# The first unit of an up projection by whole products instead of by seven half products, and other buffers for the first loads of the down projection

## The reference

```python
x = x + merged @ w_out                               # output projection
h = rms_norm(x, ffn_norm_g)
u, v = jnp.split(h @ w_up, 2, axis=-1)               # 2 x 5632 columns
u = causal_dwconv(u, conv_w, conv_b)                 # 3 taps over the tokens
x = x + (jax.nn.gelu(u) * v) @ w_down                # down projection
return rms_norm(x, final_norm_g)
```

## Time and profile before

| what | value |
|---|---|
| median of 3 runs | 2808.55 us (2808.36 to 2808.84) |
| the profiled execution, device time | 2806.89 us |
| its span in the trace | 2805.1 us |
| PE busy | 2751.3 us, 98% |
| DVE, ACT, POOL busy | 1509.0, 1008.1, 187.2 us |
| mean granted clock of TensorE | 0.992 |
| share of the chain of waits on PE | 93% |

### The profile page before, as it was taken

How to read it: one execution, slowest core, us unless ns; L and a number is a source line. 1 busy time by engine, 2 the same in 40 slices (tenths; PEclk the granted TensorE clock), 3 DMA queues, 4 the chain that set the end, 5 groups by cost and what they waited for, 6 DMA issues and landing times.

```text
span 2805.1 us, 40745 instructions
## 1 busy us (share of the span) xinstructions
PE 2751.3 (98%) x15945; PEld 2422.0 (86%) x15945; DVE 1509.0 (54%) x1831; ACT 1008.1 (36%) x1237; POOL 187.2 (7%) x156
## 2 busy tenths in 40 slices
PE   8999999999999999999989999999999998999998
PEld 6888888888888888888789999999999987888886
DVE  4445542233333433342487878787878864455454
ACT  4334432222232322132455444555554432122223
POOL 0003310000111000000000000000000000000002
PEclk9999999999999999999999999999999999999999
DMA  6532123334333233343434343535343434333332
GB/s 175 135 103 57 53 75 97 97 92 108 85 82 97 75 102 92 97 143 120 135 94 129 103 132 101 134 101 135 101 131 105 130 131 167 124 115 134 105 113 97
DMA packets 421668, 308.89 MB, mean 110 GB/s; under 512 B 6469, under 2 KB 367574, under 8 KB 420969
## 3 DMA queue, kind: packets, MB, share of 16 engines
q1 hardware_dynamic: 415351, 295.83, 36.7%
q10 hardware_dynamic: 5826, 10.76, 1.1%
q0 software_dynamic: 432, 1.50, 0.2%
HBM read 288.09 MB, written 22.06 MB: 111 GB/s over the span
## 4 chain that ended last, share of the span: by engine, by line
PE 93%; DVE 2%; issue 2%; ACT 1%; DMA 1%; SPq 0%; POOL 0%; ACTq 0%; DVEq 0%; POOLq 0%
PE bank L889 31%; PE bank L528 19%; PE bank L530 19%; PE bank L529 19%; PE bank L719 2%; PE bank L713 1%; DMA x_in<-in_x_dram 0%; DMA a_dram<-v_sb 0%; DVE ring_lo L1717 0%; ACT l_win L1081 0%; ACT l_slc L1081 0%; PE bank L769 0%; POOL l_slc L1952 0%; SPq L362 0%; PE bank L868 0%
## 5 line engine op out<-in xcount | busy, mean ns | idle before, releaser
L528 PE MATMUL bank<-h_hi,w_hi 128*128 128x512 f32 x1216 | 481.3, 396 | 2.8 <-DVE w_lo L1419 2.8
L530 PE MATMUL bank<-h_hi,w_lo 128*128 128x512 f32 x1216 | 474.6, 390 | 0.0
L529 PE MATMUL bank<-h_lo,w_hi 128*128 128x512 f32 x1216 | 474.3, 390 | 0.0
L889 PE MATMUL bank<-t_hi,ring_hi 128*128 128x256 f32 x1408 | 401.4, 285 | 18.6 <-DVE ring_lo L1717 18.6
L889 PE MATMUL bank<-t_hi,ring_lo 128*128 128x256 f32 x1408 | 400.5, 284 | 0.0
L1409 DVE TENSOR_TENSOR w_lo<-w_raw,w_hi 128x2048 fp32r<-128x2048 f32 x105 | 240.7, 2292 | 262.0 <-ACT w_hi L983 261.7
L983 ACT ACTIVATE w_hi<-w_raw 128x2048 fp32r<-128x2048 f32 x105 | 200.8, 1912 | 424.7 <-PE bank L530 420.6
L889 PE MATMUL bank<-m32r,ring_hi 128*128 128x256 f32 x1408 | 327.5, 284 | 0.0
L889 PEld LDWEIGHTS bank<-t_hi,ring_hi 128*128 128x128 f32 x1408 | 272.6, 194 | 19.6 <-issue 19.6
L528 PE MATMUL bank<-d_hi,a_hi 128*128 128x512 f32 x704 | 275.0, 391 | 7.9 <-DVE x L1889 7.9
L529 PE MATMUL bank<-d_lo,a_hi 128*128 128x512 f32 x704 | 274.7, 390 | 0.0
(11 more groups left out here) (283 smaller groups left out, 4883.1 us busy)
## 6 DMA issues: line engine op xcount, KB each, us to landing
w_raw<-in_w_in_dram SPq DMA_DIRECT2D x76, 1024.0 KB, 5.7
raw<-in_w_up_dram SPq DMA_DIRECT2D x44, 1024.0 KB, 6.9
raw<-in_w_up_dram SPq DMA_DIRECT2D x88, 512.0 KB, 6.2
d_raw<-in_w_down_dram SPq DMA_DIRECT2D x44, 1024.0 KB, 5.1
w_raw<-in_w_out_dram SPq DMA_DIRECT2D x16, 1024.0 KB, 5.1
a_dram<-v_sb SPq DMA_DIRECT2D x44, 256.0 KB, 2.0
a_in<-a_dram SPq DMA_DIRECT2D x11, 1024.0 KB, 7.4
w_raw<-in_w_branch_nsa_dram SPq DMA_DIRECT2D x8, 1024.0 KB, 5.7
```

What stands on the lines that cost most here:

```text
L528: mm(dst, l_hi, r_hi, start=first, stop=False)
L529: mm(dst, l_hi, r_lo, start=False, stop=False)
L530: return mm(dst, l_lo, r_hi, start=False, stop=final)
L889: last = mm(pb[bank][:, 0:TH], left[:, w], right[:, k, :], start=first and k == 0 and left is ring_hi[b] and right is y_hi, stop=k == KH - ...
```

## The change

- Unit 0 of the up projection becomes two whole slots, S_UP (the column of v) and S_UP + 1 (of u): 16 k-tiles by 3 matmuls of 512 columns each into banks 0 and 1. For it the whole m32 is split into h_hi and h_lo in quarters (h2_hi, h2_lo), three of them beside the last slots of the output projection. Products are now 7 x 43.
- y11, y21 and y22 are views of h_hi and h_lo. Only t1 to t4 are made by sums, and t3 and t4 lie in what is free by then. The first sum and t1's split stand beside the last output slot; the others stand in between on ScalarE and VectorE while TensorE runs unit 0 and the first products of unit 1.
- TensorE: eight k-tiles of v, the transposes of group 3, four of v, eight of u, the row scales, four of u, then the last four of each. SyncE: loads of unit 1, the two slots, then unit 2.
- The ring, the raw buffers, s_a, s_3, u_sb, v_sb, d_raw, d_hi, d_lo and the a buffers have other places. The first two quarters of x1 are loaded into buffers of their own (xs) before the last product ends.
- At the end of the up projection the piece for the last but one product comes ahead of the split of the first down slot on VectorE, and the split of the first a_in behind the last piece. The second a_in is loaded after the x1 quarters that have their own buffers.

The diff, cut to its core:

```diff
-S_DN = S_WO + 16
+S_UP = S_WO + 16
+S_DN = S_UP + 2
 UNITS = D_FF // P
-PRODUCTS = 7 * UNITS
+PRODUCTS = 7 * (UNITS - 1)
...
+    q, half = (0 if r <= 1 else 7 * r - 9), (r - 1) // 2
     if i is None:
-        return Unit(r, r, r // 2, 0 if r == 0 else 7 * r - 2)
-    return Unit(i * 4 + r, r, i * 2 + r // 2, i * 28 + (7 * r - 2))
+        return Unit(r, r, half, q)
+    return Unit(i * 4 + r, r, i * 2 + half, i * 28 + q)
...
-    h_hi = at("h_hi", 0, [P, KT, SEQ], F32R)
-    h_lo = at("h_lo", 32 * KB, [P, KT, SEQ], F32R)
+    hl = at("hl", 0, [P, 2, KT, SEQ], F32R)
+    h_hi, h_lo = hl[:, 0], hl[:, 1]
...
-    raw = [[at("raw00", A_, [P, 2, KH * P]), at("raw01", A_ + 8 * KB, [P, 2, KH * P])],
-           [at("raw10", 72 * KB, [P, 2, KH * P]), at("raw11", 88 * KB, [P, 2, KH * P])]]
-    ring_at = [A_ + 16 * KB, A_ + 24 * KB, 48 * KB, 56 * KB]
+    rs_rep2 = at("rs_rep2", A_ + 40 * KB, [P, TOK, P])
+    raw = [[at("raw00", 64 * KB, [P, 2, KH * P]), at("raw01", 72 * KB, [P, 2, KH * P])],
+           [at("raw10", A_ + 16 * KB, [P, 2, KH * P]), at("raw11", A_ + 24 * KB, [P, 2, KH * P])]]
+    ring_at = [A_ + 32 * KB, Y_, 80 * KB, 96 * KB]
     ring_hi = [at(f"ring_hi{b}", ring_at[b], [P, KH * P], F32R) for b in range(RING)]
     ring_lo = [at(f"ring_lo{b}", ring_at[b] + 4 * KB, [P, KH * P], F32R) for b in range(RING)]
-    s_a = [at(f"s_a{b}", A_ + 32 * KB + b * 4 * KB, [P, KH * P]) for b in range(2)]
-    s_3 = at("s_3", 64 * KB, [P, KH * P])
-    u_sb = at("u_sb", 68 * KB, [P, 2, SEQ])
-    v_sb = at("v_sb", 104 * KB, [P, 4, SEQ])
+    s_a = [at(f"s_a{b}", Y_ + 8 * KB + b * 4 * KB, [P, KH * P]) for b in range(2)]
+    v_sb = at("v_sb", 88 * KB, [P, 4, SEQ])
+    u_sb = at("u_sb", 104 * KB, [P, 2, SEQ])
+    s_3 = at("s_3", 108 * KB, [P, KH * P])
...
+    t1 = at("t1", A_, [P, 2, KH, TH], F32R)
     m32r = at("m32r", M_, [P, KT, SEQ], F32R)
-    y22_hi, t3_lo = m32r[:, 0:KH, 0:TH], m32r[:, 0:KH, TH:SEQ]
-    t4_lo, y22_lo = m32r[:, KH:KT, 0:TH], m32r[:, KH:KT, TH:SEQ]
     r11, r12 = m32[:, 0:KH, 0:TH], m32[:, 0:KH, TH:SEQ]
     r21, r22 = m32[:, KH:KT, 0:TH], m32[:, KH:KT, TH:SEQ]
-    d_raw = at("d_raw", A_, [P, 2, 2048])
-    d_hi = at("d_hi", 0, [P, 2, 2048], F32R)
-    d_lo = at("d_lo", 16 * KB, [P, 2, 2048], F32R)
-    a_in = [at("a_in0", 32 * KB, [P, 4, SEQ]), at("a_in1", 96 * KB, [P, 4, SEQ])]
-    a_hi = [at("a_hi0", 40 * KB, [P, 4, SEQ], F32R), at("a_hi1", 48 * KB, [P, 4, SEQ], F32R)]
-    a_lo = [at("a_lo0", 80 * KB, [P, 4, SEQ], F32R), at("a_lo1", 56 * KB, [P, 4, SEQ], F32R)]
+    t2_hi, t2_lo = m32r[:, KH:KT, TH:SEQ], m32r[:, 0:KH, 0:TH]
+    t3_hi, t3_lo = hl[:, 0, 0:KH, TH:SEQ], hl[:, 1, 0:KH, TH:SEQ]
+    t4_hi, t4_lo = m32r[:, 0:KH, TH:SEQ], m32r[:, KH:KT, 0:TH]
+    y11 = [hl[:, z, 0:KH, 0:TH] for z in range(2)]
+    y21 = [hl[:, z, KH:KT, 0:TH] for z in range(2)]
+    y22 = [hl[:, z, KH:KT, TH:SEQ] for z in range(2)]
...
+    d_raw = at("d_raw", 64 * KB, [P, 2, 2048])
+    d_hi = [at("d_hi0", A_, [P, 2048], F32R), at("d_hi1", 0, [P, 2048], F32R)]
+    d_lo = [at("d_lo0", A_ + 8 * KB, [P, 2048], F32R), at("d_lo1", 8 * KB, [P, 2048], F32R)]
+    a_in = [at("a_in0", A_ + 16 * KB, [P, 4, SEQ]), at("a_in1", 40 * KB, [P, 4, SEQ])]
+    a_hi = [at("a_hi0", Y_, [P, 4, SEQ], F32R), at("a_hi1", 16 * KB, [P, 4, SEQ], F32R)]
+    a_lo = [at("a_lo0", A_ + 24 * KB, [P, 4, SEQ], F32R), at("a_lo1", 24 * KB, [P, 4, SEQ], F32R)]
     x1 = at("x1", M_, [P, TOK, D_MODEL])
-    gfin = at("gfin", Y_, [P, D_MODEL])
-    sq3 = at("sq3", Y_ + 8 * KB, [P, 512])
+    xs = [at("xs0", Y_ + 8 * KB, [P, TOK, 512]), at("xs1", 32 * KB, [P, TOK, 512])]
...
         sp.wait_ge(w_used, S_WO + 2)
-        load_v(unit(0))
-        load_u(unit(0), 0)
-        load_u(unit(0), 1)
-        sp.wait_ge(w_ready, S_DN + 2)
         load_v(unit(1))
-        sp.wait_ge(w_used, S_DN + 2)
         load_u(unit(1), 0)
         load_u(unit(1), 1)
+        load_cols(slot(S_UP), wup, D_FF)
+        load_cols(slot(S_UP + 1), wup, 0)
+        sp.wait_ge(w_ready, S_UP + 1 + 3)
+        load_v(unit(2))
+        load_u(unit(2), 0)
+        load_u(unit(2), 1)
...
-                hold(sp, s_add, now.n * 4 + 4)
+                hold(sp, s_add, now.n * 4)
...
+        last = unit(UNITS - 1)
+        sp.wait_ge(s_add, 4 * (UNITS - 2))
         load_down(slot(S_DN), 0, 0)
-        sp.wait_ge(piece_ok, unit(43).q + 5)
+        sp.wait_ge(piece_ok, last.q + 5)
         load_down(slot(S_DN + 1), 0, 1)
+        sp.wait_ge(s_add, 4 * (UNITS - 1))
         sp.wait_ge(a_out, 16 * 8 + 64)
-        sp.wait_ge(prod_done, unit(43).q + 4)
         load_a(0, 0)
+        store_a(unit(41))
+        sp.wait_ge(piece_ok, PRODUCTS)
+        sp.wait_ge(x1_put, 80)
+        sp.dma_start(xs[0][:], x1_d[:, :, 0:512]).then_inc(x_loaded[0], 16)
+        sp.wait_ge(prod_done, PRODUCTS - 2)
+        sp.dma_start(xs[1][:], x1_d[:, :, 512:1024]).then_inc(x_loaded[1], 16)
         load_a(1, 1)
-        store_a(unit(41))
         sp.wait_ge(prod_done, PRODUCTS)
-        sp.wait_ge(x1_put, 80)
-        for j in range(4):
+        for j in range(2, 4):
...
+        up_v, up_u = slot(S_UP), slot(S_UP + 1)
+        pe.wait_ge(hl_ok, 3)
+        pe.wait_ge(x1_add, 14)
+        slot_cols(up_v, 0, range(0, 8))
         x1_transposes(3)
-        pe.wait_ge(y_part, 2)
-        product(1, 1, t1_hi, t1_lo, bank_c[0], True)
-        pe.wait_ge(y_part, 4)
-        product(2, 2, y21_hi, y21_lo, bank_b, True)
-        pe.wait_ge(y_part, 5)
-        pe.wait_ge(p1_out, 1)
-        product(3, 3, t2_hi, t2_lo, bank_a[0], False)
+        slot_cols(up_v, 0, range(8, 12))
+        slot_cols(up_u, 1, range(0, 8)).then_inc(y12_used, 1)
+        pe.wait_ge(rep2_ok, 1)
         pe.wait_ge(x1t_read, 20)
-        pe.wait_ge(rep2_ok, 1)
         for t in range(TOK):
             last = mm(pb[5][:, t * P:t * P + P], rs_rep2[:, t, :], ident[:], start=True, stop=True)
         last.then_inc(rbc2_ps, 1)
-        pe.wait_ge(y_part, 6)
-        pe.wait_ge(u2_out, 1)
-        product(4, 0, t3_hi, t3_lo, bank_a[0], False)
+        slot_cols(up_u, 1, range(8, 12))
+        pe.wait_ge(hl_ok, 4)
+        slot_cols(up_v, 0, range(12, KT))
+        slot_cols(up_u, 1, range(12, KT))
...
+            if r == 1:
+                pe.wait_ge(c21_out, 1)
+            product(now.q + 1, (b + 1) % RING, y21, bank_b, True)
             if r >= 2:
                 pe.wait_ge(c12_out, now.n - 1)
-            product(now.q + 2, (b + 2) % RING, t1_hi, t1_lo, bank_c[par], True)
+            else:
+                pe.wait_ge(y_part, 1)
+            product(now.q + 2, (b + 2) % RING, t1_, bank_c[par], True)
             pe.wait_ge(p1_out, now.n + 1)
-            product(now.q + 3, (b + 3) % RING, t2_hi, t2_lo, bank_a[par], False)
-            pe.wait_ge(c22_out, now.n)
             if r == 1:
-                pe.wait_ge(y_part, 7)
-            product(now.q + 4, b, t4_hi, t4_lo, bank_a[1 - par], False)
+                pe.wait_ge(y_part, 2)
...
+        def h2_hi(q):
+            A(h_hi[:, 4 * q:4 * q + 4, :], m32[:, 4 * q:4 * q + 4, :], ACT.Copy).then_inc(hh_ok, 1)
...
+        act.wait_ge(x1t_read, 16)
+        for sub in range(1, 4):
             hi(slot(S_WO + 12 + sub + 1))
-        m = unit(0)
+            h2_hi(sub - 1)
+            if sub == 3:
+                y_hi_part(t1[:, 0], r11, 1)
+        hi(slot(S_UP + 1))
+        for t in range(TOK):
+            square(3, t)
+        store_x1(3)
...
         wo_trans(3)
         act.wait_ge(x1t_read, 20)
-        y_hi_part(y21_hi[:, 4:8, :], m32[:, 12:16, 0:TH])
-        piece_x(2, 2, m, 0, 1)
-        y_hi_part(t2_hi[:], t_raw[:], 2)
-        piece_s(3, 3, m, s_a[0], 2)
+        h2_hi(3)
         act.wait_ge(sqrt_in, 2)
         A(nmx[:, 4:8], nmx[:, 0:4], ACT.Sqrt).then_inc(sqrt_out, 1)
         act.wait_ge(x1_put, 80)
-        y_hi_part(t3_hi[:], r12, 4)
-        p5(m, 2)
-        piece_s(4, 0, m, s_3, 4)
-        u2(m, 4)
-        m = unit(1)
-        piece_x(5, 1, m, 0, 0)
-        piece_x(6, 2, m, 0, 1)
-        act.wait_ge(rbc2_ps, 1)
-        y_hi_part(t4_hi[:], r21, 3)
-        piece_s(7, 3, m, s_a[1], 1)
-        piece_s(8, 0, m, s_a[1], 2)
-        y_hi_part(y22_hi, r22)
+        piece_x(1, 1, m, 0, 1)
+        act.wait_ge(hl_ok, 4)
+        act.wait_ge(t_add, 3)
+        y_hi_part(t2_hi, r11, 2)
...
+        act.wait_ge(w_used, S_UP + 3)
+        piece_s(2, 2, m, s_a[1], 1)
+        piece_s(3, 3, m, s_a[1], 2)
+        act.wait_ge(y12_used, 1)
+        y_hi_part(t3_hi, r12, 3)
+        act.wait_ge(y_part, 3)
+        y_hi_part(t4_hi, r21, 4)
...
+        last = unit(UNITS - 1)
+        piece_x(PRODUCTS - 2, (PRODUCTS - 2) % RING, last, 1, 1)
+        act.wait_ge(prod_done, last.q + 3)
         down_hi(slot(S_DN))
+        piece_s(PRODUCTS - 1, (PRODUCTS - 1) % RING, last, s_a[1], 3)
+        gelu(unit(UNITS - 2))
+        act.wait_ge(prod_done, last.q + 6)
         a_high(0, 0, 16)
-        period(UNITS)
-        gelu(unit(43))
+        taps(last)
+        gelu(last)
```

(87 more changed lines are left out.)

179 lines of the change are left out of this document (79 added, 100 removed).

## The result

The changed kernel takes 2792.78 us (median; 2791.70 to 2795.38), the kernel before 2808.45 us beside it on the same chip: ratio 0.9945, 95% interval 0.9928 to 0.9963, 15.7 us less (10 to 20 us by the interval). The forecast was 2791.4 us, within 2787.5 to 2798.5. The profile therefore shows 11.5 us of span where the medians show 15.7, and the first task is to see which of the two a place belongs to.

The account below looks back on a forecast made before the run. TensorE was taken as the bound, losing time only where it waits, mainly for VectorE. 12.6 us (up projection start) + 6.0 (down passage) - 1.5 (clock) = 17.1 us, from 2808.55 to 2791.4 us; range 2787.5 to 2798.5.

Parts of the forecast that it names:

- Unit 0: Start of up projection: seven products removed (20.19 us), 96 matmuls of 512 columns added (21.78 us), cost +1.6 us.
- the walk: Engine queues stepped in order from the output projection's end to unit 2's first product at 1429.6; gain 12.6 us.
- What stands beside it: Unit 0's splits and sums on ScalarE and VectorE: early splits covered by the output projection, later ones stall unit 1.
- Forecast stalls of 1.7, 1.0 and 2.6 us: Unit 1, products 1, 3 and 4: waits for unit 0's second bank, ScalarE's copy of product 0, and s_3 with its split.
- The price of a missing cover: Output projection: without its cover for the moved splits, unit 0's first matmul would be late by up to 4 us.
- The clock: Half-speed matmuls behind short gaps of 2.2, 2.4 and 2.6 us: bounds none and three stretches, one taken, 1.5 us.
- the step to the mark: Start of the up projection and its products: gain 12.6 us, with 1.5 us taken off separately for the clock.
- The passage: Up to down projection: earlier pieces and x1 loads bring the third down slot 6.0 us earlier; bounds 2 and 8.
- The term that was mis-sized: Passage: 17.5 us of queue from 2296.8, a's last store landing about 2315, third down slot 12.3 us later.
- the freed buffers: Passage: buffers for x1's first two quarters and the second a_in free earlier, so the queue flows from 2295.2 on.
- Rival B: Passage: second a_in load moved into the full queue, last store of a lands as before; gain 11.1, 2797.4; chance 0.12.
- The loop: Up projection's loop: no repeated gap; VectorE busy 40.11 of 50 us, about 4 us to spare per unit.

Follow-up runs that it names:

- e7: Changed kernel with VectorE and ScalarE reordered at unit 1: unit 0's banks read first, fourth token sum's low split after the sum for piece 8; 2787.11 us, ratio 0.9923.
- e5: Changed kernel with the splits of h's first three quarters moved out from under the output projection, behind the up projection's first weight split; 2799.88 us.
- e8: The changed kernel itself, unedited, run again beside other runs on the same chip (also e8_unchanged); 2792.25 us.
- e9: Changed kernel with three reorderings together: unit 1's queues, a_in split first, weight loads of third and fourth down slots early; 2776.41 us, ratio to before 0.9885.
- e10: Kernel before, with its buffers, unit 0 and loads, but the last two pieces made ahead of and between the down projection's first splits; 2804.37 us, ratio 0.9984.
- e1: Changed kernel with x1's first two quarters loaded only after the last product, the second a_in ahead of them; 2793.17 us, ratio to before 0.9949.
- e3: Changed kernel with the first a_in's split ahead of unit 42's gelu on ScalarE and its last tap on VectorE; 2791.32 us, ratio 0.9941.
- e11: The changed kernel itself, unedited, run again beside the version with all three reorderings (also e11_unchanged); 2793.30 us.
- e4: Changed kernel with unit 0's bank read-outs first and the fourth token sum's split behind the piece for product 6; 2790.99 us, ratio 0.9937.
- e2: Changed kernel with third and fourth down slots' weight loads issued ahead of x1's last quarters and the wait for a's stores; 2785.19 us, ratio 0.9921.
- e6: Changed kernel with VectorE's old order restored for one step: first down weights' low split before the last-but-one product's piece; 2790.63 us, ratio 0.9942.

## Why the prediction was right, point by point

**Unit 0: right, to 0.4 us.** Between the end of the output projection and product 0 the walk had 25.4 us; 24.98 were measured. The step of a 512-column matmul is unchanged (24 from 1386.58 to 1392.03: 0.227 us), and the stall ahead of the token-sum matmuls was 0.29 us for 0.2. The Trainium skill's "Wait — 56ns, not 53.3ns?" (TensorE: Matmul & The Clock Gate) makes such a matmul 215.7 ns; the rows of both kernels disagree with it by 11 ns.

**What stands beside it: the order was right, and its cost 0.2 to 0.4 us more.** Forecast stalls of 1.7, 1.0 and 2.6 us ahead of products 1, 3 and 4; measured 2.10, 0.78, 2.49. The last two are ended by the operations named. For the first the profile names no releaser, but VectorE's read of the second bank of unit 0 ends at 1416.60, 0.10 us ahead of the matmul. From the end of the output projection product 4 starts at 42.5 us, where the walk had 42.1. A slip of 0.2 us in the walk goes the other way: product 4 from 1426.5 on ends at 1429.4, not 1429.6, so its own steps give 12.8 us and not 12.6. e7 shows that these stalls were what the order of VectorE's and ScalarE's queues made of the edit. The price of a missing cover was wrong: up to 4 us, measured 5.9 and half clock behind it (e5).

**The clock: one stretch of 1.5 us forecast, one of 1.4 to 1.5 found** on the path to the mark. With it the step to the mark is closed: 12.6 less 0.2 to 0.4 for the walk and 1.4 to 1.5 for the clock is the 10.9 of the table. That it was one is luck: the prediction had no row for it and chose between none and three, and in the profile of e8 the same kernel has its slow stretch at another place (last section). A second stretch, of 1.7 us, lies in the first two down slots (2292.01 to 2315.66, 23.65 us for 96 matmuls, 21.95 in e9, where the clock is full); it costs nothing, because the third slot waits for its load anyway. A third, behind the gap ahead of the third slot, stood in before too and is now 0.8 us dearer; the forecast had not looked at it.

**The passage: 6.0 forecast, 4.1 found, and of two causes one was false.** The gaps of 2.2, 1.0 and 2.4 us came as 2.20, 0.89 and 2.46. The queue started when it was said to (8.0 us after the mark for 7.7) and was full for 16.9 us for 17.5; the weights went from issue to matmul in 12.46 us for 12.3. The Trainium skill, DMA: Bandwidth & Descriptors, "Where 436 GB/s comes from", names about 358 GB/s; the windows have up to 407, and over the 16.9 us the queue moved 6.57 MB, 389 GB/s, with this one core running. The term that was mis-sized is what lies between the full queue's end and the next issue: put at 0.7 us, measured 2.7. Windows of before, where the full queue ends at about 2320.1, its last packet at 2320.5, and the load goes out at 2321.07, 0.9 to 1.0 behind the full queue:

```profile
2319.50:2320.00 0.50, 0.50 (x4) 0.42 (x3) 0.00 (x0) 0.00 (x0) 0.00 (x0) 1.00 1.06 393
2320.00:2320.50 0.50, 0.50 (x4) 0.38 (x4) 0.00 (x0) 0.00 (x0) 0.00 (x0) 1.00 0.29 107
```

In after 0.9 us stand behind the last packet (0.5 in before, 0.6 in e10), and one DMA engine trails the others by 1.8 us ahead of them. The trail is in the runs of the changed kernel (e1: the full queue ends at 2302.2, the last packet at 2303.8, the load goes out at 2304.70; 1.5 to 1.9 us of trail in e3 to e8 and e11 too) and short in the two kernels with the old buffers (0.5 us in before; e10: 2316.0, 2316.8, 2317.36). So the load went out 27.7 us after the mark, not 25.9, and that is the 1.8 us of the difference.

What makes the trail was not tried, and it need not be the moved tiles. In each of the nine profiles with the long trail one packet of 16 KiB on the queue for instructions falls into the full queue (e3: 2295.84 to 2296.95), and in before and e10 it falls outside (2298.19 and 2320.00 in before). Around it e3's share of the sixteen DMA engines falls from 1.05 to 0.98, as if one of them did nothing else; the third line is the packet's count in after, from 2300 to 2305:

```profile
2294.00:2295.80 1.80, 1.80 (x10) 1.49 (x9) 1.15 (x1) 0.61 (x1) 0.93 (x2) 1.00 1.05 388
2295.90:2296.90 1.00, 1.00 (x6) 0.81 (x5) 1.00 (x2) 0.00 (x0) 0.00 (x0) 1.00 0.98 375
q8 instruction: 1, 0.02, 1.4%
```

The packet takes 1.1 us, about what the trail has grown by. At the end of the span it is the same again: in all eleven profiles of the changed kernel a packet of 8 KiB for instructions falls among the last output stores, which then land 0.6 us later, and in before and e10 it comes ahead of the first of them. That one takes 0.3 us, half of the 0.6. That these packets, and not the buffers, make both trails is likely by this, not shown.

What failed in reasoning is the credit. The step argued with the freed buffers, from which the queue starts earlier; e1 and e10 show that this start is eaten by the a_in load that moved into the queue (one load of 2.7 us against a start 3.2 us earlier leaves the 0.5 to 0.6 us of e1), while the earlier end of the products does the rest. Rival B named this very mechanism, and its mechanism is true; its price was wrong, since it supposed that the store would land when it did before, though the products end 5.2 us earlier. The sum came out near because both halves of the passage were in one term, and that is luck. Nor could the time alone have told the two apart: the interval, 10 to 20 us, holds rival B's 11.1 as well as the forecast's 17.1.

**What was not in the forecast.** The half clock behind the third slot's gap took 0.8 us more in this profile than in that of before. The output stores took 0.6 us more in every profile of the changed kernel. The output projection ended 2.1 us later; e11, the same kernel, has 0.2 us earlier instead. So the 15.7 us of the medians lie nearer to the forecast's 17.1 than the 11.5 of the one profile.

**The loop: as said.** No repeated gap; TensorE is busy 50.00 of 50 us, VectorE 39.46:

```profile
1650.00:1700.00 50.00, 50.00 (x419) 50.00 (x418) 39.46 (x44) 26.26 (x32) 3.35 (x3) 1.00 0.38 103
```

## What to carry to other kernels

Where an engine in the middle (VectorE here) feeds the bound one, walk its queue in order and write down who waits for each item: most of what was lost here was a split that nobody needed yet standing ahead of one that somebody did, and moving it needed no new buffer. A prefetch into a queue that would be full anyway was worth only the time by which the whole queue started earlier, less whatever moved into it; the wait in front of the next load, here for stores to which that load had no relation, was worth more than all of it. Before a gap is counted as a gain, ask whether the next wait has an end of its own: 2.5 us were worth nothing with that wait there (e3) and came in full once it was gone (e9).

## What the runs showed of the hardware

The execution of the same code differs, among others, in one place far ahead of the edit. In the window from 195 to 205 us, in the attention, these are e8_unchanged and e11_unchanged, the same kernel:

```profile
195.00:205.00 10.00, 8.90 (x42) 7.58 (x41) 6.20 (x25) 6.32 (x12) 0.00 (x0) 0.83 0.01 2
```

```profile
195.00:205.00 10.00, 8.90 (x49) 7.45 (x48) 7.50 (x33) 7.66 (x17) 0.17 (x1) 1.00 0.03 3
```

With a mean granted clock of 0.83 (a part of the ten us at 1.2 GHz, the rest at 2.4) the transposes start at 1391.39, with 1.00 at 1389.78. Seven of the profiles have 0.83 (after, e3, e4, e7 to e10) and six 1.00 (before, e1, e2, e5, e6, e11), and from 196 to 205 us each of the seven loses 1.6 us against the six. Of the 2.1 us by which the profile of after starts its up projection late, 1.6 arise there and 0.5 in the first 45 us: the VectorE operation that is at 195.95 in before is at 196.46 in after, and one at 203.74 is at 205.82. The times of one and the same kernel lie 2 to 4 us apart, so this is a part of their spread only. What decides between the two was not tried.

A gap of 1.8 to 2.5 us can be followed by matmuls at 1.2 GHz: behind the 1.79 us in e4, behind the 2.49 us in after, and behind the longer 5.89 in e5. The same gap need not be: of the eight profiles with a gap of 2.0 to 2.1 us at product 1, six have the half clock behind it (e8 and e6 among them) and two don't (after and e11). Each such stretch cost 1.4 to 3.0 us where it lay on the path (3.0 in the third down slot of after; 1.4 to 1.5 behind the 2.49 us gap of after, over half of the gap itself), and that is why e2, e5, e7 and e9 moved the time by more than the gaps that they added or removed.

The trail of one DMA engine behind a queue that is otherwise full had not been expected either: 1.5 to 1.9 us in the nine profiles with a packet for instructions in the full queue, 0.5 to 0.8 in the two without.
